# A softmax scale moved into the query norm, and a row maximum written out already negated

## The chip, the cores and the metric

The kernel runs on one core of one Trainium2 chip. The metric is the device time of one execution in microseconds (us). The profiled execution is one of its own, with its own time; the engines are named as in the profile: PE is TensorE (PEld its weight loads), DVE is VectorE, ACT is ScalarE, POOL is GpSimd, and SP issues most DMAs.

## The reference, cut to what matters

The model is two layers of a hybrid backbone on 256 latent and 256 context tokens of width 1024. Each layer has an input projection, four branches (Fourier, convolution, pooling, attention), a gated merge and an output projection, and then a feed-forward part (dense in layer 0, top 2 of 8 experts in layer 1). The change is in the attention branch alone:

```python
def rmsnorm(x, g):
    y = xf * lax.rsqrt(jnp.mean(xf * xf, axis=-1, keepdims=True) + EPS)
    return (y * g.astype(jnp.float32)).astype(x.dtype)
...
q = rmsnorm(proj[..., OFF_Q:OFF_K].reshape(b, l, N_HEADS, HEAD_DIM), q_norm_g)   # 8 heads of 64
...
def gqa_attend(qg, k, v):
    s = jnp.einsum('bqkgd,bskd->bkgqs', qg, k).astype(jnp.float32) * (HEAD_DIM ** -0.5)
    p = jax.nn.softmax(s, axis=-1).astype(v.dtype)
    return jnp.einsum('bkgqs,bskd->bqkgd', p, v)
```

Latent queries attend to 512 keys (256 latent, 256 context), context queries (layer 0 only) to the 256 context keys.

## The kernel before, in words

Every engine has one instruction stream, written out by hand in program order, and the streams meet through semaphores. Activations lie transposed (channels on partitions, tokens along the free dimension). The order of a layer's attention half is: norm1, the projections k, v, q0 to q3, F, ca, the head norms (`heads0` for k, `heads1` to `heads4` for q), more projections, rotary embedding, Fourier and pooling products, the duplication of the keys, then the attention units, then the four branches with their gates (`project("gate...")`, lines 556 to 558, and line 668), then the output projection. The eight PSUM banks are taken in a fixed rotation: `psum_order` writes down which result comes next, and a matmul that opens a bank waits until what lay in it eight places earlier has been read.

Head norm: PE sums the squares of a head (line 582), ACT takes the square root of mean plus eps (line 1012), DVE takes the reciprocal and multiplies q or k by it and by the gain (line 1355 and the two lines after it).

An attention unit is one head and one block of 128 query rows. There are 32 units in layer 0 (16 with 512 keys, then 16 with 256 keys) and 16 in layer 1 (all with 512 keys). For unit u:

- PE computes the scores S(u) into a bank (line 509). Units are issued in pairs. The two heads of a pair sit on different halves of the array's rows.
- DVE takes the row maximum (line 1410) into column 3 of a small tile `stat[:, u % 4]`, waits for its own result (`step`, a semaphore that DVE raises and waits for itself), multiplies it by -1/8 into column 0 (line 1411), and raises `negmax_ready`.
- ACT computes exp(S/8 + column 0) into `prob` or `root`, a ring of four buffers, with the row sum beside it (line 1040; the read of the accumulator is a second instruction).
- DVE takes the reciprocal of the row sum (line 1416), waits for itself, and scales the row (line 1417).
- PE transposes the row in blocks, T(u) (line 517). ACT copies the result to `pT` (line 1030, `keep_turned`).
- After four units PE multiplies by the values, V(v) (line 528), and DVE copies the result to `attnT` (line 1424, `keep_values`).

DVE's order is maximum(u), normalise(u - 1), and after every fourth unit keep_values. ACT's order is exp(u) and one keep_turned for each unit. PE's order is a pair of S, a V every second pair, a pair of T. The order of banks makes the second S of the pair that is issued after a V wait until DVE has copied that V out.

Constants lie in one tile `const`, whose columns are `ones`, `eps`, `ident`, `heads` and so on. It is loaded in two DMAs, the columns up to `eps` early and the rest later.

Of the kernel before, what the change touches and what calls it, by code (L numbers as in the profile page):

```python
# [16 lines left out]
ALU = mybir.AluOpType  # L17
ACT = mybir.ActivationFunctionType
AX = mybir.AxisListType.X
# [46 lines left out]

CONST = {}
_at = 0
for _name, _n in (("ones", P), ("eps", 1), ("ident", P), ("heads", P), ("rot", P), ("dup0", P), ("dup1", P), ("chan_cos", P),
                  ("chan_sin", P), ("pair", 2), ("below", P), ("iota", P), ("iota8", 8), ("seq", 2 * 512),  # L70
                  ("cos", LAT), ("sin", LAT)):
    CONST[_name] = (_at, _at + _n)
    _at += _n
# [50 lines left out]
def build(nc, xT_in, consts_in, pool_in, vec_in, cond_in, rows_in, router_in, first_in, mod_in, attn_in, ffn13_in, ffn2_in, moe_up_in, moe_down_in, out):  # L124
    with ExitStack() as ctx:
# [135 lines left out]
        def C(name):  # L261
            a, b = CONST[name]
            return const[:, a:b]
# [633 lines left out]
        def _(act):  # L897
# [96 lines left out]
            def attention_half(layer):  # L994
                N = T if layer == 0 else LAT
                if layer:
                    for n in range(2):
                        split(layer, n)
                norm(layer, "norm1", T)
                split(layer, 2)  # L1000
                for name in ("k", "v", "q0", "q1", "q2", "q3", "F0", "F1", "ca0", "ca1"):
                    if name in ("k", "q0", "q1", "q2", "q3"):
                        t = 0 if name == "k" else int(name[1]) + 1
                        n = T if t == 0 else N
                        b = filled(act, layer, name)
                        fn(hsq[:, t, 0:n], b[:, 0:n], ACT.Square).then_inc(S("head_square_ready"), 1)
                        fn(qk[:, t, 0:n], b[:, 0:n], ACT.Copy).then_inc(free(layer, name), 1)
                    split(layer, TILE_NO[name] + TILE_RING)
                for t in range(5):
                    n = T if t == 0 else N  # L1010
                    b = filled(act, layer, f"heads{t}")
                    fn(hsq[:, t, 0:n], b[:, 0:n], ACT.Sqrt, bias=C("eps"), scale=1.0 / HD) \
                        .then_inc(free(layer, f"heads{t}"), 1)
                for c in range(2):
                    b = filled(act, layer, f"cg{c}")
                    fn(sg[:, c, 0:N], b[:, 0:N], ACT.Sigmoid).then_inc(free(layer, f"cg{c}"), 1)
                    split(layer, TILE_NO[f"cg{c}"] + TILE_RING)
                for c in range(2):
                    split(layer, TILE_NO[f"P{c}"] + TILE_RING)

                units = attention_units(layer)

                def keep_turned(u):
                    s, g, qt, j = units[u]
                    n = 4 - 2 * s
                    v = u // 4
                    if j == 0 and v >= 2:
                        filled(act, layer, f"V{v - 2}")
                    b = filled(act, layer, f"T{u}")
                    fn(pT[:, v % 2, 0:n, j, :], b[:, 0:n * P].rearrange("p (c q) -> p c q", q=P), ACT.Copy) \  # L1030
                        .then_inc(free(layer, f"T{u}"), 1)

                for u in range(len(units) + 4):
                    if u % 2 and u >= 4:
                        keep_turned(u - 4)
                    if u < len(units):
                        n = T if units[u][0] == 0 else CTX
                        nxt("negmax_ready")
                        b = filled(act, layer, f"S{u}")
                        fn(probs[u % 4][:, 0:n], b[:, 0:n], ACT.Exp, bias=stat[:, u % 4, 0:1], scale=HD ** -0.5,  # L1040
                           accum_out=stat[:, u % 4, 1:2]).then_inc(free(layer, f"S{u}"), 1)
                    if u % 2 and 3 <= u < len(units) + 3:
                        keep_turned(u - 3)

                step = 0
                for i in BRANCH_ORDER:
                    if i == 1:
                        act.wait_ge(S("conv_summed"), layer + 1)
                        for c in range(2):
                            fn(csq[:, c, 0:N], conv[:, c, 0:N], ACT.Square).then_inc(S("conv_square_ready"), 1)  # L1050
                        b = filled(act, layer, "convnorm")
                        fn(root[:, 0:N], b[:, 0:N], ACT.Sqrt, bias=C("eps"), scale=1.0 / 256) \
                            .then_inc(free(layer, "convnorm"), 1)
                        for c in range(2):
                            nxt("conv_normed")
                            fn(conv[:, c, 0:N], conv[:, c, 0:N], ACT.Silu).then_inc(S("conv_ready"), 1)
                    for j in range(KD):
                        if step == 0:
                            act.wait_ge(S("conv_gated"), 2 * layer + 2)
                        if step >= 2:  # L1060

                            pi, pj = BRANCH_ORDER[(step - 2) // KD], (step - 2) % KD
                            read(act, layer, f"branch{pi}{pj}")
                        b = filled(act, layer, f"gate{i}{j}")
                        fn(sg[:, step % 2, 0:N], b[:, 0:N], ACT.Sigmoid).then_inc(free(layer, f"gate{i}{j}"), 1)  # L1065
                        split(layer, TILE_NO[f"gate{i}{j}"] + TILE_RING)
                        step += 1
                norm(layer, "norm2", N)
# [121 lines left out]
        def _(dve):  # L1190
# [137 lines left out]
            def attention_half(layer):  # L1328
# [78 lines left out]
                def maximum(u):  # L1407
                    n = T if units[u][0] == 0 else CTX
                    b = filled(dve, layer, f"S{u}")
                    step(dve.tensor_reduce(stat[:, u % 4, 3:4], b[:, 0:n], AX, ALU.max))  # L1410
                    ts(stat[:, u % 4, 0:1], stat[:, u % 4, 3:4], -HD ** -0.5, None, ALU.mult).then_inc(S("negmax_ready"), 1)

                def normalise(u):
                    n = T if units[u][0] == 0 else CTX
# [298 lines left out]
def constants():  # L1713

    c = np.zeros((P, CONST_LEN), np.float64)

    def put(name, a):
        c[:a.shape[0], CONST[name][0]:CONST[name][1]] = a

    i = np.arange(P)  # L1720
    put("ident", np.eye(P))
    put("ones", np.ones((P, P)))
    put("heads", (i[:, None] // HD == i[None, :] // HD).astype(float))

    rot = np.zeros((P, P))
    for out_c in range(P):
        rot[out_c + 16 if out_c % 32 < 16 else out_c - 16, out_c] = -1.0 if out_c % 32 < 16 else 1.0
    put("rot", rot)
    for g in range(NKV):
        d = np.zeros((P, P))  # L1730
        d[HD * g + i % HD, i] = 1.0
        put(f"dup{g}", d)
    ch = np.outer(np.arange(64), np.arange(64)) * (2 * np.pi / 64)
    eye2 = np.eye(2)
    norm = 1.0 / np.sqrt(64.0 * LAT)
    put("chan_cos", np.kron(eye2, np.cos(ch)) * norm)
    put("chan_sin", -np.kron(eye2, np.sin(ch)) * norm)
    put("pair", np.tile(np.eye(2), (2, 1)))
    put("below", (i[:, None] < i[None, :]).astype(float))
    put("iota", np.tile(i[None, :], (P, 1)))  # L1740
    put("iota8", np.tile(E - np.arange(E)[None, :], (P, 1)))
    put("eps", np.full((P, 1), EPS))
    t = np.outer(np.arange(LAT), np.arange(LAT)) % LAT * (2 * np.pi / LAT)
    s = np.concatenate([np.cos(t), np.sin(t)], axis=1).reshape(2, P, 512)
    put("seq", s.transpose(1, 0, 2).reshape(P, 1024))
    n_freq = HD // 4
    freqs = (10000.0 ** (-np.arange(n_freq) / n_freq)).astype(np.float32)
    tok = np.arange(LAT)
    where = np.where((i % HD < 32)[:, None], (tok // GRID_W)[None, :], (tok % GRID_W)[None, :])
    angle = where.astype(np.float32) * freqs[i % 16][:, None]  # L1750
    put("cos", np.cos(angle.astype(np.float64)))
    put("sin", np.sin(angle.astype(np.float64)))

    m = np.zeros((2, 2, P, 2, LAT))
    for g, w in enumerate(WINDOWS):
        full = np.zeros((LAT, LAT))
        for o in range(LAT):
            lo, hi = max(o - w // 2, 0), min(o + w // 2, LAT)
            full[lo:hi, o] = 1.0 / (hi - lo)
            full[o, o] -= 1.0  # L1760
        m[g // 2, :, :, g % 2, :] = full.reshape(2, P, LAT)
    pool = m.transpose(2, 0, 1, 3, 4).reshape(P, POOL_LEN)
    return c.astype(np.float32), pool.reshape(P, 2, 2, LAT * 2).astype(np.float32)
# [98 lines left out]
```

## Time and profile before

| | |
|---|---|
| median of 3 runs | 2235.92 us (2235.74 to 2236.14) |
| profiled execution: time | 2234.71 us |
| profiled execution: span, first to last instruction | 2232.9 us |
| mean granted TensorE clock over the span | 0.98 of full speed |
| instructions | 27842 |

The time of the profiled execution is its span and 1.8 us around it. A busy share is an average over stages. Which engine sets the pace of a stage is read from the chain of waits, which is followed back from the last instruction, and from the order of time on each engine. The granted clock is given as a share of 2.4 GHz, so 0.5 is 1.2 GHz.

### The profile page before, as it was taken

What the parts mean: (1) busy time and instruction counts of PE and PEld (TensorE: products, weight loads), DVE (VectorE), ACT (ScalarE), POOL (GpSimd) and SP (SyncE); (2) the same over time, 40 slices, a digit from 0 to 9 for tenths busy, and PEclk for the clock granted to TensorE, in tenths of its full rate; (3) what the DMA queues carried; (4) which work ended last, traced back from release to release, by engine and by line L of the source; (5) the groups of instructions that cost most, each with busy time, mean ns of one, the idle gap of its engine ahead of it and who ended that gap; (6) DMA issues with size and microseconds to landing.
All of it is one profiled execution on the core that took longest, in us unless ns stands there. A gap on an engine that the chain in (4) does not pass through costs nothing.

```text
span 2232.9 us, 27842 instructions
## 1 busy us (share of the span) xinstructions
PE 2135.7 (96%) x9866; PEld 1710.4 (77%) x9866; DVE 1713.1 (77%) x2158; ACT 1120.7 (50%) x1276; POOL 42.5 (2%) x84
## 2 busy tenths in 40 slices
PE   8989999998999999779997999999999999999997
PEld 6765776655788888667987888888888888888886
DVE  7777687646767766777745988988898988889895
ACT  3316221213333332434334777767777777767774
POOL 0000000000000000000000000000000000000000
PEclk9999999999999999899997999999999999999999
DMA  7500244343444443222444899989899999989993
GB/s 316 198 24 1 95 175 141 123 151 113 154 166 170 159 159 133 94 72 78 177 165 188 348 368 346 371 329 371 333 362 359 350 349 350 372 324 368 336 375 118
DMA packets 77284, 512.38 MB, mean 229 GB/s; under 512 B 8738, under 2 KB 9890, under 8 KB 22820
## 3 DMA queue, kind: packets, MB, share of 16 engines
q1 hardware_dynamic: 65700, 469.59, 55.9%
q0 software_dynamic: 11520, 41.95, 5.4%
q8 instruction: 38, 0.62, 0.1%
q14 instruction: 26, 0.21, 0.0%
HBM read 510.46 MB, written 1.05 MB: 229 GB/s over the span
## 4 chain that ended last, share of the span: by engine, by line
PE 88%; DVE 8%; ACT 2%; issue 2%; DMA 1%; SPq 0%; DVEq 0%; ACTq 0%
PE bank L807 9%; PE bank L805 9%; PE bank L806 9%; PE bank L556 5%; PE bank L558 5%; PE bank L557 5%; PE bank L668 5%; PE bank L826 5%; PE bank L828 5%; PE bank L827 5%; PE bank L678 4%; PE bank L724 2%; PE bank L725 2%; PE bank L726 2%; PE bank L700 2%; PE bank L710 2%
## 5 line engine op out<-in xcount | busy, mean ns | idle before, releaser
L934 ACT ACTIVATE down_high<-W 128x1024 fp32r<-128x1024 f32 x224 | 237.1, 1064 | 139.3 <-PE bank L828 139.2
L1275 DVE TENSOR_TENSOR up_b_low<-W,up_b_high 128x2048 fp32r<-128x2048 f32 x112 | 256.5, 2290 | 56.5 <-ACT up_b_high L927 56.5
L1282 DVE TENSOR_TENSOR down_low<-W,down_high 128x1024 fp32r<-128x1024 f32 x224 | 271.8, 1223 | 31.8 <-ACT down_high L934 22.5
L556 PE MATMUL bank<-h_high,tile_high 128*128 128x512 f32 (+1 forms) x704 | 259.7, 369 | 11.7 <-DVE tile_low L1326 11.7
L1269 DVE TENSOR_TENSOR up_a_low<-W,up_a_high 128x2048 fp32r<-128x2048 f32 x112 | 255.8, 2284 | 1.9 <-ACT up_a_high L921 1.9
L558 PE MATMUL bank<-h_high,tile_low 128*128 128x512 f32 (+1 forms) x704 | 239.3, 340 | 0.0
L557 PE MATMUL bank<-h_low,tile_high 128*128 128x512 f32 (+1 forms) x704 | 239.2, 340 | 0.0
L921 ACT ACTIVATE up_a_high<-W 128x2048 fp32r<-128x2048 f32 x112 | 212.9, 1901 | 2.1 <-PE bank L807 2.1
L927 ACT ACTIVATE up_b_high<-W 128x2048 fp32r<-128x2048 f32 x112 | 213.2, 1903 | 0.0
L826 PE MATMUL bank<-down_high,mact_high 128*128 128x512 f32 x448 | 186.4, 416 | 2.6 <-DVE down_low L1282 2.6
L828 PE MATMUL bank<-down_low,mact_high 128*128 128x512 f32 x448 | 176.3, 393 | 0.0
L805 PE MATMUL bank<-up_a_high,gathered_high 128*128 128x512 f32 x448 | 174.5, 390 | 1.4 <-DVE gathered_low L1603 1.4
L827 PE MATMUL bank<-down_high,mact_low 128*128 128x512 f32 x448 | 175.4, 392 | 0.0
L807 PE MATMUL bank<-up_b_low,gathered_high 128*128 128x512 f32 x448 | 175.0, 391 | 0.0
L805 PE MATMUL bank<-up_b_high,gathered_high 128*128 128x512 f32 x448 | 174.4, 389 | 0.3 <-DVE up_b_low L1275 0.3
L807 PE MATMUL bank<-up_a_low,gathered_high 128*128 128x512 f32 x448 | 174.3, 389 | 0.0
L806 PE MATMUL bank<-up_b_high,gathered_low 128*128 128x512 f32 x448 | 174.3, 389 | 0.0
L806 PE MATMUL bank<-up_a_high,gathered_low 128*128 128x512 f32 x448 | 174.3, 389 | 0.0
L556 PEld LDWEIGHTS bank<-h_high,tile_high 128*128 128x128 f32 x704 | 135.6, 193 | 35.2 <-DVE tile_low L1326 12.6
L1065 ACT ACTIVATE sg<-bank 128x512 f32<-128x512 f32 (+1 forms) x64 | 31.4, 490 | 261.2 <-PE bank L558 261.1
L557 PEld LDWEIGHTS bank<-h_low,tile_high 128*128 128x128 f32 x704 | 135.7, 193 | 21.9 <-issue 7.9
L558 PEld LDWEIGHTS bank<-h_high,tile_low 128*128 128x128 f32 x704 | 135.5, 192 | 14.7
(229 smaller groups left out, 4087.7 us busy)
## 6 DMA issues: line engine op xcount, KB each, us to landing
W<-in_moe_up SPq DMA_DIRECT2D x224, 1024.0 KB, 6.0
W<-in_moe_down SPq DMA_DIRECT2D x112, 1024.0 KB, 4.9
W<-in_w_mod_later POOLq DMA_DIRECT2D x80, 512.0 KB, 3.7
W<-in_ffn SPq DMA_DIRECT2D x33, 1024.0 KB, 4.8
W<-in_attn_blocks SPq DMA_DIRECT2D x24, 1280.0 KB, 5.9
W<-in_attn_blocks SPq DMA_DIRECT2D x22, 1024.0 KB, 5.2
W<-in_attn_blocks SPq DMA_DIRECT2D x8, 1536.0 KB, 7.1
shift_tiles<-in_w_mod_first SPq DMA_DIRECT2D x8, 512.0 KB, 13.9
```

The lines of the kernel that those rows point to most:

```text
L556: mm(b[:, 0:n], wh[:, r, k, :], hh[:, k, 0:n], start=k == 0, stop=False)
L557: mm(b[:, 0:n], wh[:, r, k, :], hl[:, k, 0:n], start=False, stop=False)
L558: last = mm(b[:, 0:n], wl[:, r, k, :], hh[:, k, 0:n], start=False, stop=k == KD - 1)
L805: mm(b[:, :], hgh[:, k, :], high[u][:, kk, :], start=k == 0, stop=False)
L806: mm(b[:, :], hgl[:, k, :], high[u][:, kk, :], start=False, stop=False)
L807: last = mm(b[:, :], hgh[:, k, :], low[u][:, kk, :], start=False, stop=k == KD - 1)
L826: mm(b[:, :], mah[:, u, a], ch[:, h, w], start=start and h == 0, stop=False, skip_group_check=True)
L827: mm(b[:, :], mal[:, u, a], ch[:, h, w], start=False, stop=False, skip_group_check=True)
L828: last = mm(b[:, :], mah[:, u, a], cl[:, h, w], start=False, stop=stop and h == 1, skip_group_check=True)
L1269: tt(al[u][:], raw_a[u].rearrange("p (k n) -> p k n", k=KD // 2), ah[u][:].bitcast(F32), ALU.subtract) \
L1275: tt(bl[u][:], raw_b[u].rearrange("p (k n) -> p k n", k=KD // 2), bh[u][:].bitcast(F32), ALU.subtract) \
L1282: tt(cl[:, h, :], raw_c[u][:, h * D:(h + 1) * D], ch[:, h, :].bitcast(F32), ALU.subtract) \
```

## The change

The factor 1/8 on the scores is taken into the queries. For the four q tiles the square root is taken of the sum of squares plus 64 eps, in place of the sum over 64 plus eps, which makes its reciprocal smaller by the factor 8. For this a constant column `eps_q` is added behind `eps`, so all constants behind it move by one column, and the second of the two DMAs of `const` is one column longer. The exponential has no scale any more. The row maximum is written negated by the reduction itself; the multiplication behind it and DVE's wait on its own semaphore between the two are gone. That is one instruction fewer for each of 48 units.

```diff
-for _name, _n in (("ones", P), ("eps", 1), ("ident", P), ...
+for _name, _n in (("ones", P), ("eps", 1), ("eps_q", 1), ("ident", P), ...
...
                 for t in range(5):
                     n = T if t == 0 else N
                     b = filled(act, layer, f"heads{t}")
-                    fn(hsq[:, t, 0:n], b[:, 0:n], ACT.Sqrt, bias=C("eps"), scale=1.0 / HD) \
+                    fn(hsq[:, t, 0:n], b[:, 0:n], ACT.Sqrt, bias=C("eps_q" if t else "eps"), scale=1.0 if t else 1.0 / HD) \
                         .then_inc(free(layer, f"heads{t}"), 1)
...
-                        fn(probs[u % 4][:, 0:n], b[:, 0:n], ACT.Exp, bias=stat[:, u % 4, 0:1], scale=HD ** -0.5,
+                        fn(probs[u % 4][:, 0:n], b[:, 0:n], ACT.Exp, bias=stat[:, u % 4, 0:1],
                            accum_out=stat[:, u % 4, 1:2]).then_inc(free(layer, f"S{u}"), 1)
...
-                    step(dve.tensor_reduce(stat[:, u % 4, 3:4], b[:, 0:n], AX, ALU.max))
-                    ts(stat[:, u % 4, 0:1], stat[:, u % 4, 3:4], -HD ** -0.5, None, ALU.mult).then_inc(S("negmax_ready"), 1)
+                    dve.tensor_reduce(stat[:, u % 4, 0:1], b[:, 0:n], AX, ALU.max, negate=True).then_inc(S("negmax_ready"), 1)
...
+    put("eps_q", np.full((P, 1), HD * EPS))
```

## Rows read from the trace of the kernel before

**Rows 1.** The page: busy time, share of the span, instructions of three engines.

```profile
PE 2135.7 (96%) x9866; PEld 1710.4 (77%) x9866; DVE 1713.1 (77%) x2158; ACT 1120.7 (50%) x1276; POOL 42.5 (2%) x84
```

**Rows 2.** The page: the chain that ended last, by engine.

```profile
PE 88%; DVE 8%; ACT 2%; issue 2%; DMA 1%; SPq 0%; DVEq 0%; ACTq 0%
```

**Rows 3.** Windows: start:end, length, busy us (count) by engine, PE clock, DMA share, GB/s.

```profile
163.00:212.00 49.00, 42.68 (x260) 23.56 (x257) 39.08 (x136) 34.97 (x97) 0.00 (x0) 1.00 0.01 1
997.00:1028.00 31.00, 26.15 (x159) 14.88 (x156) 22.58 (x67) 21.53 (x49) 0.00 (x0) 0.94 0.00 1
```

**Rows 4.** Timeline of DVE, layer 0, a unit of 512 keys: start, us, engine, line, operation.

```profile
166.50 0.68 DVE L1410 TENSOR_REDUCE stat<-bank 128x1 f32<-128x512 f32 x1
167.22 0.15 DVE L1411 TENSOR_SCALAR stat<-stat 128x1 f32<-128x1 f32 x1
167.29 0.15 DVE L1416 RECIPROCAL stat<-stat 128x1 f32<-128x1 f32 x1
167.48 0.49 DVE L1417 TENSOR_SCALAR prob<-prob,stat 128x512 f32<-128x512 f32 x1
167.88 0.68 DVE L1410 TENSOR_REDUCE stat<-bank 128x1 f32<-128x512 f32 x1
```

**Rows 5.** Chain of waits, layer 0, up to the first V: start, us, what.

```profile
166.59 0.61 DVE stat L1410
...
172.11 0.61 DVE stat L1410
...
173.71 0.50 ACT pT L1030
```

**Rows 6.** Chain of waits, layer 0, from the first V to the end.

```profile
179.50 1.99 PE bank L509 x4
...
206.17 0.16 DVE stat L1411
...
208.94 0.94 ACT pT L1030 x3
```

**Rows 7.** Timeline of DVE, layer 0: a copy of V, then a unit of 256 keys.

```profile
179.89 0.41 DVE L1424 COPY attnT<-bank 128x256 f32<-128x256 f32 x1
180.23 0.68 DVE L1410 TENSOR_REDUCE stat<-bank 128x1 f32<-128x512 f32 x1
...
191.59 0.42 DVE L1410 TENSOR_REDUCE stat<-bank 128x1 f32<-128x256 f32 x1 [0.84 <-PE bank L509]
...
192.12 0.15 DVE L1416 RECIPROCAL stat<-stat 128x1 f32<-128x1 f32 x1
```

**Rows 8.** Timeline of ACT, layer 0, three instructions in a row.

```profile
183.99 0.60 ACT L1030 ACTIVATE pT<-bank 128x512 f32<-128x512 f32 x1 [0.70 <-PE bank L517]
184.48 0.68 ACT L1040 ACTIVATE prob<-bank,stat 128x512 f32<-128x512 f32 x1
...
185.14 0.60 ACT L1030 ACTIVATE pT<-bank 128x512 f32<-128x512 f32 x1
```

**Rows 9.** Timeline of PE, layer 0 and then layer 1: eight blocks of T in each.

```profile
176.32 1.09 PE L517 MATMUL bank<-const,prob 128*128 128x128 f32 x8
...
1002.16 2.03 PE L517 MATMUL bank<-const,prob 128*128 128x128 f32 x8
1004.12 1.60 PE L509 MATMUL bank<-kdup,qk 64*128 64x512 f32 x4
```

**Rows 10.** Windows, layer 1, columns as in rows 3.

```profile
1002.00:1006.00 4.00, 4.00 (x17) 2.28 (x16) 3.79 (x13) 3.31 (x9) 0.00 (x0) 0.61 0.00 0
```

**Rows 11.** Timeline of DVE, then chain of waits, both of layer 1.

```profile
1005.76 0.69 DVE L1410 TENSOR_REDUCE stat<-bank 128x1 f32<-128x512 f32 x1
...
1019.96 0.16 DVE stat L1411
```

**Rows 12.** Instructions by line: duration ns min/median/max, first and last start, forms.

```profile
L647 PE MATMUL bank<-qk,const x8: 379/523/592, 397.7 to 1125.7; 128*128 128x512 f32 x4, 128*128 128x256 f32 x4
L582 PE MATMUL bank<-hsq,const x20: 379/592/592, 101.8 to 958.0; 128*128 128x512 f32 x12, 128*128 128x256 f32 x8
```

More of the change, by code:

```diff
@@ L68 @@
 _at = 0
-for _name, _n in (("ones", P), ("eps", 1), ("ident", P), ("heads", P), ("rot", P), ("dup0", P), ("dup1", P), ("chan_cos", P),
+for _name, _n in (("ones", P), ("eps", 1), ("eps_q", 1), ("ident", P), ("heads", P), ("rot", P), ("dup0", P), ("dup1", P), ("chan_cos", P),
                   ("chan_sin", P), ("pair", 2), ("below", P), ("iota", P), ("iota8", 8), ("seq", 2 * 512),
```

## The prediction

> **What bounds the kernel now.** I read the page first. PE is busy for 96% of the span and DVE for 77% [rows 1], and the chain that ended last runs over PE for 88% and over DVE for 8% [rows 2]. So a faster DVE is worth only what it saves in stretches where the chain runs over the changed instructions. These run in two stretches alone, layer 0 from 163 to 212 us and layer 1 from 997 to 1028 us, 80 us of 2232.9 [rows 3]. In neither is an engine full: PE is busy 42.68 of 49 us and DVE 39.08 [rows 3]. The question is therefore which engine is late at each joint, and for that I went to the timeline of each engine and to the chain of waits within the two stretches.
>
> **What one unit saves on DVE.** In steady state the reduction starts at 166.50, the multiplication at 167.22, the reciprocal at 167.29, the scaling of the row at 167.48 and the next reduction at 167.88, which makes a period of 1.38 us [rows 4]. The multiplication starts 0.04 after the reduction has ended (166.50 + 0.68 = 167.18), because DVE waits for its own result. An instruction that waits for nothing starts before the one ahead of it has ended: the reciprocal 0.08 early (167.22 + 0.15 = 167.37 against 167.29), the reduction 0.09 early [rows 4], and behind a copy out of PSUM 0.07 early (179.89 + 0.41 = 180.30 against 180.23) [rows 7]. After the change the reciprocal of unit u - 1 stands directly behind the reduction of unit u and does not depend on it. From start to start that is 0.79 now and will be 0.68 - 0.08 = 0.60: 0.19 us less. For 256 keys it is 192.12 - 191.59 = 0.53 now [rows 7] and 0.42 - 0.08 = 0.34 after, again 0.19. No row shows a reduction with a waitless successor, so I bound this from both sides. At the least the slot of the multiplication goes, 167.29 - 167.22 = 0.07. At the most 0.79 - 0.60 and a little more, 0.23, if the successor could start 0.12 early. I take 0.19, by the nearest row, the copy out of PSUM. The path to ACT gains about as much: from the start of the reduction to the end of the multiplication it is 0.87 now and will be 0.68, and the wait behind it stays, which I count as 0.18.
>
> The Trainium skill has a rule that speaks against this size. VectorE: DVE Perf Modes, section The DRAIN you can't avoid, says that an instruction costs its pipeline flush with or without a semaphore, and that the semaphore itself costs nothing extra. By that rule the removed wait is worth nothing, and the sum would be the 1.1 us of the first rival below. The rows here differ: 0.04 late with the wait, 0.07 to 0.09 early without [rows 4, 7]. The same page says elsewhere that an instruction which isn't held starts earlier.
>
> **Where the segment is on the path, layer 0.** From the end of the ACT table load the chain is DVE's own loop. Five reductions stand on it before the first V, the first at 166.59 and the last at 172.11 [rows 5]. The last hands over to ACT, whose copy at 173.71 releases V [rows 5]. Savings: 4 x 0.19 + 0.18 = 0.94. DVE's period becomes 1.38 - 0.19 = 1.19. ACT must keep up: copy to exp takes 184.48 - 183.99 = 0.49 and exp to copy 185.14 - 184.48 = 0.66, together 1.15 [rows 8]. That is just under 1.19, so ACT is next in line but not yet the bound. PE needs for two units, without a V, some 1.06 for a pair of S and 1.09 for eight blocks of T [rows 9], 2.15 against DVE's 2.38, and is hidden too.
>
> From the first V on PE is the bound for most of each group of four units, and DVE sits idle for 0.84 us in each [rows 7]. But the chain crosses DVE once in every group. The pair of S that comes after V takes 1.99 at 179.50 where a pair takes 1.06 [rows 6], because its second half waits for the bank that DVE empties with the copy at 179.89 [rows 7]. That copy stands behind the reduction, the multiplication, the reciprocal and the scaling of the row. Each such crossing gives 0.19. There are five (V1 to V5): 0.95. V6 is released over DVE's line 1411 (206.17 [rows 6]) and ACT: 0.17. V7 is released by three ACT copies at 208.94 [rows 6] and gives nothing. Layer 0: 0.94 + 0.95 + 0.17 = 2.06.
>
> **Layer 1.** The loop before the first V looks the same but is not. PE's clock is at half there: 0.61 between 1002 and 1006 [rows 10], a stretch at 1.2 GHz that follows PE's long wait for the first row. Eight blocks of T take 2.03 us in place of 1.09, and the next pair of S 1.60, without a gap between them [rows 9], and the reduction at 1005.76 has just waited for that pair [rows 11]. What DVE gains earlier is lost in waiting for PE. Only the last segment, from that reduction over ACT to V0, keeps its 0.18. V1 has the crossing of layer 0 (0.19), V2 is released over line 1411 (1019.96 [rows 11]) and ACT (0.18), V3 by ACT alone. Layer 1: 0.55.
>
> **The other edits.** The square root and the exponential keep their instruction, shape and count, with other constants: 0. I see no row with such a constant changed; a table with another cost would be the only way, and both take their scale as an immediate before and after. The constants move from odd to even columns. `heads` (now odd, column 257) is multiplied in at most 592 ns and `ones` (even, column 0), in the same shape, in at most 592 ns [rows 12], so I take 0 between ends of -0.1 and +0.1 us. The DMA of the constants grows by one column in 2698, 0.04% of it, and all DMAs together are 1% of the chain, 22 us [rows 2]: under 0.01 us. No wait is added, no transfer is moved. After attention the chain is PE's own gate projections, so what is saved moves everything behind it forward by as much.
>
> **Sum.** 2.06 + 0.55 = 2.61 us, 14 segments of 48. The profiled execution took 2234.71, so 2232.1 by its own measure. It lies 1.21 under the median of the runs, 2235.92, so the forecast is **2233.3 us**.
>
> **Rivals.**
> - *Only the slot is won.* If a successor of the reduction starts no earlier than the multiplication does now, each segment gives 0.07 to 0.08: 14 x 0.075 = 1.05, so 2234.9. For it: a reduction may keep its pipe longer than a copy. Against it: three different pairs of rows all start early [rows 4, 7].
> - *The clock falls elsewhere.* PE waits as long for the first row in layer 0, with the clock at 1.00 throughout [rows 3]. If the stretch at half clock comes in both layers, layer 0 loses four of its five first steps, 0.76: 2234.1. If it comes in neither, layer 1 gains them: 2232.5. Everything behind layer 0 also runs 2 us earlier, and the other half-clock stretches may come out a little longer or shorter, about a microsecond either way.
> - *DVE was the pace all along.* 48 x 0.19 = 9.1, so 2226.8. Against it: DVE's idle 0.84 [rows 7] and the copies of ACT on the chain [rows 6].
> - *The reduction gets slower by the negation.* This is the one way to the other side. Place: line 1410. Price, if a second pass is made: (0.68 - 0.42) / 256 [rows 4, 7] is 1.0 ns an element, 0.52 us for 512 keys and 0.26 for 256. Net of the 0.19 it is +0.33 and +0.07. Layer 0: 5 x 0.33 before the first V, 2 x 0.33 and 4 x 0.07 after; layer 1: 5 x 0.33, as DVE then is slower than PE even at half clock, and 2 x 0.33. That is 2.6 + 2.3 = 4.9, so 2240.8. It decides from a reduction of 0.68 + 0.19 = 0.87 us on. Nothing in the trace shows a negated reduction.
>
> **Chances.** The forecast 0.60, only the slot 0.12, the clock 0.12, DVE all along 0.04, slower 0.04, nothing 0.08. The range of 8 in 10 goes from 2230.9 (0.23 a segment is 3.2, no half clock in layer 1 another 0.8, one later half-clock stretch shorter by 1.0) to 2236.0 (only the slot and one such stretch longer, or nothing arrives). This kernel's runs can tell a change of about 0.2%, that is 4.5 us: faster means under 2231.4, slower over 2240.4. Faster: 0.04 from DVE all along and 0.04 from the low ends of the forecast and the clock, 0.08. Slower: 0.04. Within: 0.88.
>
> **What would show it.** Right: no row on line 1411's place, the reduction still at 0.68 and 0.42, a period of 1.19 before the first V of layer 0, the reciprocal 0.60 behind the start of the reduction, V0 of layer 0 about 0.94 earlier against the first exp, V to V shorter by 0.19, ACT nearly without gaps in the first loop, and layer 1 shorter by 0.5. Wrong: a reduction over 0.7 us, a first loop with a period of 1.3 or more, a stretch at 0.5 of the clock within 163 to 212 us, or a difference behind the attention that isn't the shift alone.

## The result, and the profile after

The changed kernel takes 2229.98 us (median of 9 runs, 2228.42 to 2230.91), the kernel before 2235.74 us on the same chip (9 runs, 2233.26 to 2237.15). The ratio is 0.9976, with a 95% interval of 0.9967 to 0.9985: 5.8 us less, where 2.6 were forecast. The time lies under the range. The profiled execution took 2230.79 us, with a span of 2229.0, against 2234.71 and 2232.9 before.

On VectorE the change does to the rows what the working said. The page of the kernel after, busy time and the chain by engine, against rows 1 and 2:

```profile
PE 2137.6 (96%) x9866; PEld 1714.5 (77%) x9866; DVE 1706.0 (77%) x2110; ACT 1119.7 (50%) x1276; POOL 42.6 (2%) x84
...
PE 89%; DVE 7%; ACT 2%; issue 1%; DMA 1%; SPq 0%; DVEq 0%; ACTq 0%
```

DVE has 48 instructions fewer and 7.1 us less to do. The timeline of DVE in layer 0, the same unit as in rows 4 (line 1415 is now the reciprocal, 1416 the scaling of the row):

```profile
165.95 0.68 DVE L1410 TENSOR_REDUCE stat<-bank 128x1 f32<-128x512 f32 x1
166.55 0.15 DVE L1415 RECIPROCAL stat<-stat 128x1 f32<-128x1 f32 x1
166.74 0.49 DVE L1416 TENSOR_SCALAR prob<-prob,stat 128x512 f32<-128x512 f32 x1
167.14 0.69 DVE L1410 TENSOR_REDUCE stat<-bank 128x1 f32<-128x512 f32 x1
```

The negated reduction still takes 0.68 us, the reciprocal starts 0.60 behind it, and the period is 1.19 against 1.38 [rows 4]. So the size of one segment, 0.19 us, was right. The difference lies elsewhere: in where the clock fell and in the loop over the experts. The chain of waits of the kernel before (start, us, what) is shown at its first S and last V of each layer and its first V of layer 0, at the gathers (the products that collect an expert's tokens, line 760) for the second and the third expert, and at the last one:

```profile
162.62 1.11 PE bank L509 x3
...
174.44 1.95 PE bank L528 x16
...
210.12 1.08 PE bank L528 x8
...
996.30 1.11 PE bank L509 x3
...
1026.07 1.95 PE bank L528 x16
...
1329.56 3.57 PE bank L760 x32
...
1454.61 3.57 PE bank L760 x32
...
2204.93 3.57 PE bank L760 x32
```

The same of the kernel after:

```profile
162.07 1.11 PE bank L509 x3
...
173.74 1.95 PE bank L528 x16
...
208.30 1.08 PE bank L528 x8
...
994.43 1.11 PE bank L509 x3
...
1023.60 1.95 PE bank L528 x16
...
1327.32 3.57 PE bank L760 x32
...
1452.12 3.57 PE bank L760 x32
...
2200.96 3.57 PE bank L760 x32
```

From the first S to the last V, layer 0 takes 46.23 us in place of 47.50 (1.27 less, 2.06 expected) and layer 1 29.17 in place of 29.77 (0.60 less, 0.55 expected). Then comes what the prediction does not have. One turn of the loop over the experts takes 1452.12 - 1327.32 = 124.80 us and took 125.05 before. The change touches none of its instructions. Over the seven turns that can be read, from the second gather to the last, that is 1.73 us. If the first expert gains as much, it is 2.0 over eight; its own stretch can't show it, as a half-clock stretch of the router reaches into it (before, a granted clock of 0.61 from 1211 to 1214 us, with the first gather at 1209.60).

The 3.92 us between the two profiled executions are these: 0.55 ahead of the first S, where the change has nothing that it should shorten, 1.27 in layer 0's attention, 0.60 in layer 1's, 1.73 in the seven turns, and -0.23 in all the rest.

Layer 0 lost its first steps to the clock. A window of the kernel after, columns as in rows 3, just as T and S of the first units run:

```profile
166.00:170.00 4.00, 3.91 (x16) 2.29 (x16) 3.82 (x11) 2.83 (x8) 0.00 (x0) 0.63 0.00 0
```

The granted clock is 0.63 there, so part of these 4 us ran at 1.2 GHz; in the first profile of the kernel before it was 1.00 throughout layer 0's attention [rows 3]. PE had waited for the first row just before, 2.03 us against 2.04 there. The prediction named such a stretch as a sign of being wrong; it belongs to its rival on the clock.

### The profile page after: what moved, and what is told of

Same layout as the page of the kernel before. It is cut to its first block, busy times and chain, and to the rows that moved or that the text cites. A ratio compares the mean times of both kernels' runs of the same rounds, so it can differ in the third digit from the quotient of the medians.

```text
span 2229.0 us, 27794 instructions
## 1 busy us (share of the span) xinstructions
PE 2137.6 (96%) x9866; PEld 1714.5 (77%) x9866; DVE 1706.0 (77%) x2110; ACT 1119.7 (50%) x1276; POOL 42.6 (2%) x84
## 4 chain that ended last, share of the span: by engine, by line
PE 89%; DVE 7%; ACT 2%; issue 1%; DMA 1%; SPq 0%; DVEq 0%; ACTq 0%
PE bank L805 9%; PE bank L807 9%; PE bank L806 9%; PE bank L556 5%; PE bank L557 5%; PE bank L558 5%; PE bank L668 5%; PE bank L826 5%; PE bank L828 5%; PE bank L827 5%; PE bank L678 4%; PE bank L724 2%; PE bank L725 2%; PE bank L726 2%; PE bank L709 2%; PE bank L699 2%
```

## The experiments

Below, "one expert" is the time between two gathers in a chain of waits. Theory A: the gain beyond the attention comes from the constants, which moved from odd to even columns. Theory B, the rival: the place of the constants does nothing, and the rest is the phase of the loop (how its waits fall against each other), or chance. The first four kernels tell these apart.

**e1, only the columns moved.** The kernel before with an unused `eps_q` behind `eps`.

```diff
-("ones", P), ("eps", 1), ("ident", P), ("heads", P), ...
+("ones", P), ("eps", 1), ("eps_q", 1), ("ident", P), ("heads", P), ...
```

> The kernel before with the column eps_q added behind eps and not used: every constant behind it moves from an odd to an even column, nothing else changes. Measured is 5.8 us less for the whole change, while the attention stretches account for 1.9 us in the trace and the loop over the experts for 1.8 us (125.05 us for one expert before, 124.80 after). Theory A (the constants' columns make PE's transposes in the expert loop a little faster): 125.05 becomes about 124.80, the run 1.5 to 3 us shorter than before. Theory B (the place of the constants does nothing; the rest is phase and scatter): within 0.7 us of before, one expert still takes 125.05.

2233.49 us against 2235.82, ratio 0.9988 (0.9979 to 0.9997). Its chain of waits, the same two gathers:

```profile
1330.29 3.57 PE bank L760 x32
...
1455.09 3.57 PE bank L760 x32
```

124.80 us for one expert, with all of VectorE's work unchanged. Theory A holds and B falls for this part: by the runs the columns alone are worth 2.3 us (0.7 to 4.7), by the seven turns in the trace 1.73.

**e2, the change without the move.** `eps_q` as the last constant.

```diff
-("eps", 1), ("eps_q", 1), ("ident", P), ...
+("eps", 1), ("ident", P), ...
...
-("cos", LAT), ("sin", LAT)):
+("cos", LAT), ("sin", LAT), ("eps_q", 1)):
```

> The whole change, but with eps_q as the last constant, so that all others keep their odd columns. Theory A: only the attention's part is left, 2 to 3 us less than before (2233), and one expert takes 125.05 us. Theory B: like the change itself, 5 to 6 us less (2230), and 124.80 us for one expert, if that comes from the removed instructions by way of the phase in which the loop runs.

2231.81 us, ratio 0.9983 (0.9974 to 0.9992): 4.0 us less, more than theory A's 2 to 3, with a wide interval. One expert takes 125.05 us again (1326.60 and 1451.65 in its chain). So the columns decide the loop and not the removed instructions.

**e12, the same kernel once more**, because of that interval.

> The change with eps_q as the last constant, once more, as the first time gave a wide interval (2231.8, 4.0 us less than before). By the terms read from the traces it should give 1.9 to 3.3 us in the attention stretches and up to 0.7 in the router's stage, 2.0 us less than the change itself with its moved constants: 2231.5 to 2233.

2231.78 us against 2235.24, ratio 0.9987 (0.9978 to 0.9996). In both sets of runs the negated reduction by itself is worth 3.5 to 4 us, with intervals that reach from 0.9 to 5.8. The chain of waits of e12, layer 1's first S and last V, then the output projection and the first gather:

```profile
995.22 1.11 PE bank L509 x3
...
1023.60 1.95 PE bank L528 x16
...
1156.01 27.91 PE bank L678 x128
...
1206.34 5.85 PE bank L760 x32
```

Layer 1's attention takes 28.38 us here, 1.39 less than before, as the half clock does not fall within it. The stage of the router, from the output projection to the first gather, takes 50.33 where the kernel before needs 51.11 (1158.49 to 1209.60). No instruction in it has changed. Both chains are alike up to the router's first products, 33.18 us into the stage. The first of these, and the window of 2 us around it, in the kernel before and then in e12:

```profile
1191.67 0.99 PE bank L737 x4
```

```profile
1191.60:1193.60 2.00, 1.93 (x10) 1.96 (x11) 2.00 (x6) 2.00 (x6) 0.00 (x0) 0.50 1.00 418
```

```profile
1189.19 0.58 PE bank L737 x4
```

```profile
1189.10:1191.10 2.00, 1.91 (x14) 1.94 (x14) 2.00 (x6) 2.00 (x6) 0.00 (x0) 0.74 1.01 426
```

Before, these products run at half clock from the first on. In e12 the clock is still at 1.00 for the first of them (1189 to 1190 us) and falls behind it. PE has waited for ScalarE just ahead in both, 3.56 and 3.57 us. After 1.4 us of such products e12 is 0.79 ahead, and 0.78 at the end of the stage. But what layer 0 saves (46.30 in place of 47.50) is not in this profile's total, as a table further down shows.

**e3 and e4, the change and the kernel before once more.**

> The change once more, unaltered, as the yardstick for the other runs on this chip: theory B's scatter would let its expert period and its half-clock stretch in layer 0's attention come out otherwise than in the first profile; if both are fixed by the kernel, the profile shows 124.80 us again. Time 2230 +- 1.

> The kernel before, unaltered, timed against itself: within 0.7 us of before by every theory. It shows in a second profile whether 125.05 us for one expert and the clock at full speed throughout layer 0's attention belong to the kernel or to one execution.

e3: 2230.08 us, ratio 0.9975 (0.9966 to 0.9984). e4: 2235.10 us, ratio 0.9998 (0.9989 to 1.0007). One expert takes 124.80 and 125.05 us again: both belong to the kernels. The half clock in layer 0's attention does not. In e4 the window from 166 to 170 us shows 0.58 in a kernel that had 1.00 in its first profile. V0 stands 11.92 us behind the first S in place of 11.82, so the half clock costs the kernel before next to nothing there, where DVE sets the pace.

These two and the kernels of the other experiments show what the stretches outside the attention do. Microseconds between marks of the chains of waits (start of the first S, start of the last V, second gather, last gather):

| | before | e4 | after | e3 | e12 | e10 | e7 |
|---|---|---|---|---|---|---|---|
| up to the first S | 162.62 | 162.04 | 162.07 | 161.47 | 161.35 | 161.64 | 163.55 |
| attention, layer 0 | 47.50 | 47.61 | 46.23 | 46.29 | 46.30 | 46.32 | 45.45 |
| up to layer 1's first S | 786.18 | 786.22 | 786.13 | 787.49 | 787.57 | 787.53 | 786.29 |
| attention, layer 1 | 29.77 | 29.68 | 29.17 | 28.53 | 28.38 | 29.69 | 28.53 |
| up to the second gather | 303.49 | 304.27 | 303.72 | 302.81 | 302.88 | 304.30 | 302.70 |
| seven experts | 875.37 | 875.37 | 873.64 | 873.65 | 875.38 | 875.37 | 873.93 |

In e3, e12 and e10 the stretch between the two attentions is 1.3 us longer than in the kernel before, and what layer 0's attention had saved is gone when layer 1's begins. In these three the granted clock is 0.57 or 0.58 both from 404 to 412 and from 985 to 989 us; the kernel before has 0.74 and 1.00 there, e4 0.81 and 0.61. No instruction in that stretch has changed. That the clock makes the difference is read from its place and not tested. The time up to the first S differs by up to 2.2 us as well.

**e5 and e6, which constant.** One unused column on both sides of `ident` (e5), or behind it (e6), in the kernel before.

```diff
-("eps", 1), ("ident", P), ("heads", P), ...
+("eps", 1), ("pad0", 1), ("ident", P), ("pad1", 1), ("heads", P), ...     # e5
+("eps", 1), ("ident", P), ("pad0", 1), ("heads", P), ...                  # e6
```

> The kernel before, with one unused column ahead of ident and one behind it: ident moves to an even column (130), all other constants stay at odd ones. Theory A1 (PE's transposes in the expert loop read ident, and its column decides): one expert takes 124.80 us as in the two kernels with all constants moved, the time is about 2 us less than before. Theory A2 (another constant decides): 125.05 us, no difference.

> The kernel before, with one unused column behind ident: ident stays at column 129, all constants behind it move to even columns. Theory A1 (ident decides): 125.05 us for one expert and no difference in time (within 0.8 us). Theory A2: 124.80 us and about 2 us less.

e5: 2233.62 us against 2235.00, ratio 0.9991 (0.9982 to 1.0001). e6: 2234.95 us, ratio 0.9997 (0.9988 to 1.0007). The two times are near the limit of what can be told. The traces are not. The two gathers in the chains of e5, then of e6:

```profile
1330.25 3.57 PE bank L760 x32
...
1455.05 3.57 PE bank L760 x32
```

```profile
1329.85 3.57 PE bank L760 x32
...
1454.90 3.57 PE bank L760 x32
```

124.80 with `ident` alone moved, 125.05 with all the others moved. The constants' tile is as long in e6 as in e1 (124.80), so it isn't its length either. It is the column of `ident` that counts, and the only reader of `ident` in the seven turns is line 814, PE's transposes. The other profiles agree: the ten kernels and repeats with `ident` at column 129 take 875.4 us each for seven experts, the five with it at column 130 873.6. In the runs the same step is 1.7 us between e2 and e3, taken together, and 1.6 between e14 and e13 below.

**e7, the change with `ident` on a multiple of 64 bytes** (14 more unused columns).

> The change, with 14 unused columns behind eps_q, so that ident starts at column 144, a multiple of 64 bytes, instead of 130. If only odd or even counts: 124.80 us for one expert and the time of the change (2230.0 +- 0.7). If coarser alignment counts too, less than 124.80 us for one expert, and each 0.1 us there makes 0.8 us in all.

2229.50 us, ratio 0.9971 (0.9959 to 0.9983), 124.85 us for one expert: nothing more from the coarser alignment, and no faster than the change within the intervals. But this profile has the clock at 1.00 from 166 to 170 us. Its chain, first S, first V and last V of layer 0:

```profile
163.55 1.11 PE bank L509 x3
...
174.44 1.95 PE bank L528 x16
...
209.00 1.08 PE bank L528 x8
```

V0 stands 10.89 us behind the first S, 0.93 less than before (0.94 expected), and the whole takes 45.45 in place of 47.50: 2.05 less, where the prediction has 2.06. From the third unit on the chain before V0 runs over ACT, with a copy every 1.19 us (170.12, 171.32, 172.51), so ACT is level with DVE here, and a still faster DVE would win nothing in this loop.

**e15, a second identity for the expert loop alone**, at an even column at the end of the constants, in the kernel before.

```diff
-mprod[:, u, h * P:(h + 1) * P], C("ident"))
+mprod[:, u, h * P:(h + 1) * P], C("ident2"))
```

> The kernel before with a second identity at an even column (2828) at the end of the constants, read only by the transposes in the expert loop (line 814); all others read the old one at column 129. Theory A1 in its narrow form (the transposes of the expert loop alone pay for the odd column): one expert 124.80 us and the run about 2 us less than before. If another reader of ident pays: 125.05 us.

2234.36 us against 2234.99, ratio 1.0000 (0.9990 to 1.0009), and 124.95 us for one expert (1328.07 and 1453.02 in its chain). That is between the two values, so neither form of the theory is met. Line 814 alone, in a window of 245 us of the loop (PE busy, then its weight loads, clock, DMA share, GB/s), in the kernel before, e5 and e15:

```profile
1460.00:1705.00 245.00, 10.30 (x54) 7.54 (x54) 1.00 0.93 352
```

```profile
1460.00:1705.00 245.00, 10.24 (x54) 7.46 (x54) 1.00 0.92 352
```

```profile
1460.00:1705.00 245.00, 10.26 (x54) 7.46 (x54) 1.00 0.92 353
```

The weight loads of the transposes are as short in e15 as in e5. So the transposes do pay for the odd column, but they are the smaller part. An expert is 14 turns of an inner loop, and a turn is 18 ns shorter in e5 than before. By the starts of PE's products between 1460 and 2200 us some 6 of these lie at the two transposes of a turn (108.3 ns from one to the next in place of 110.5), in e15 too (108.4). The other 12 or so lie between the products of the down projection behind them (lines 826 to 828), which don't read `ident`; in e15 they gain only 1. The second identity also moves everything behind the constants by 129 columns, rounded. Why those products follow the column of `ident`, and why not in e15, stays open.

**e8, the scale alone.** The maximum taken plainly, then multiplied by -1.

```diff
-dve.tensor_reduce(stat[:, u % 4, 0:1], b[:, 0:n], AX, ALU.max, negate=True).then_inc(S("negmax_ready"), 1)
+step(dve.tensor_reduce(stat[:, u % 4, 3:4], b[:, 0:n], AX, ALU.max))
+ts(stat[:, u % 4, 0:1], stat[:, u % 4, 3:4], -1.0, None, ALU.mult).then_inc(S("negmax_ready"), 1)
```

> Half of the change: the scale goes into the query norm (square root with eps_q, exponential without a scale), but the maximum is taken plainly and multiplied by -1 on VectorE in a second instruction, as before. eps_q is the last constant, so no constant moves. All theories: the norm and the exponential cost what they cost, so DVE's period before the first V is 1.38 us, the steps from V to V are those of before (6.97, 6.55, 5.72, 5.28, 4.42, 4.06 us in layer 0), the time is within 0.8 us of before. If it is shorter by over 1 us, the scale itself pays in a way that I missed.

2235.22 us, ratio 1.0002 (0.9992 to 1.0011), DVE's period 1.38 us. Square root and exponential with other constants cost nothing that shows, as predicted.

**e9, the wait kept, the multiplication gone.**

```diff
 dve.tensor_reduce(stat[:, u % 4, 0:1], b[:, 0:n], AX, ALU.max, negate=True).then_inc(S("negmax_ready"), 1)
+done_max[0] += 1
+dve.wait_ge(S("negmax_ready"), done_max[0])
```

> The change without the multiplication but with VectorE's wait kept: behind the negated reduction VectorE waits for that reduction's own semaphore before it goes on. eps_q is the last constant, so the constants stay at odd columns. Theory W (the wait costs most of the 0.19 us): only the slot of the multiplication is saved, the reciprocal starts 0.72 us behind the start of the reduction, DVE's period before the first V is 1.31 us, each step from V to V is 0.07 us shorter than before and not 0.19, the attention gives 1.0 us in all. Theory N (a wait on one's own semaphore costs nothing, as the Trainium skill's page VectorE: DVE Perf Modes, section The DRAIN you can't avoid, has it): 1.19 us and 0.19 as in the change.

The timeline of DVE in layer 0 (lines shifted by up to 3):

```profile
165.76 0.68 DVE L1411 TENSOR_REDUCE stat<-bank 128x1 f32<-128x512 f32 x1
166.48 0.16 DVE L1418 RECIPROCAL stat<-stat 128x1 f32<-128x1 f32 x1
166.68 0.49 DVE L1419 TENSOR_SCALAR prob<-prob,stat 128x512 f32<-128x512 f32 x1
167.08 0.69 DVE L1411 TENSOR_REDUCE stat<-bank 128x1 f32<-128x512 f32 x1
```

The reciprocal starts 0.72 behind the reduction, the period is 1.32. So of 0.19 us the multiplication's slot makes 0.06 and the wait on its own semaphore 0.13. The Trainium skill's VectorE: DVE Perf Modes, section The DRAIN you can't avoid, has it, measured on a chain of copies, that such a semaphore costs nothing extra; by the rows here it cost 0.13 us each. The attention stretches are 0.83 and 0.40 us shorter than before (161.81 to 208.48, 991.63 to 1021.00), 1.2 together, about the 1.0 expected.

The time, though, is 2229.73 us, ratio 0.9976 (0.9966 to 0.9986): 5.5 us less, with the constants at odd columns and 125.05 us for one expert. Neither theory had that.

**e14 and e13, the same once more, and with `eps_q` behind `eps`.**

> The negated reduction with VectorE's own wait kept and the constants at odd columns, a second time. If the placement of the half-clock stretches belongs to the kernel: 2229.7 +- 0.7 again, and the stretch near 560 us is 3.4 us long and not 6.8, and two of 6.8 stand between 900 and 920 where other kernels have 3.4, 3.4 and 6.8. If it was luck: 2234 to 2234.6, 1.0 us less than before.

> The negated reduction with VectorE's own wait kept, now with eps_q behind eps as in the change, so that ident is at its even column. By sums: the kernel with the wait and odd columns took 5.4 us less than before, though its attention stretches are only 1.2 us shorter; its trace lays the rest on half-clock stretches that fall elsewhere. If that placement belongs to the kernel and survives a start that is a little different, 2.0 us come on top for the expert loop (124.80 us each): 2227.7, faster than the change. If it was the luck of one set of executions, about 2232.5 (2235.4 - 1.0 - 2.0).

e14: 2230.53 us against 2234.99, ratio 0.9984 (0.9975 to 0.9993). The gain, 4.5 us, is less than the first time but more than the attention's 0.9 (0.50 and 0.37 in this profile). The placement is as the first theory had it: the granted clock is 0.50 from 559.1 to 562.3 and back at 1.00 from 562.6 on, and 0.50 throughout 900.6 to 907.1 and 910.8 to 917.3. e13: 2228.91 us, ratio 0.9975 (0.9965 to 0.9985), between what its two theories expected. The gain is not the luck of one set. From the last V of layer 0 to the first S of layer 1, where no instruction differs, e9 takes 783.15 us, e14 and e13 781.69 each, the kernel before 786.18 and 786.22. The chain of waits of the kernel before, from the last product of the third branch over the wait for the norm of the convolution to the output projection; then of e14:

```profile
394.40 3.45 PE bank L668 x8
...
408.65 3.78 PE bank L668 x4
...
465.54 55.22 PE bank L678 x128
```

```profile
392.89 3.45 PE bank L668 x8
...
407.14 1.98 PE bank L668 x4
...
461.11 55.22 PE bank L678 x128
```

And two windows of each, the kernel before first:

```profile
408.00:411.00 3.00, 2.35 (x3) 1.18 (x4) 0.00 (x0) 2.97 (x4) 0.00 (x0) 0.50 0.02 5
411.00:416.00 5.00, 5.00 (x14) 3.39 (x13) 3.43 (x4) 0.45 (x1) 0.00 (x0) 0.64 0.00 0
```

```profile
408.00:411.00 3.00, 3.00 (x12) 2.07 (x11) 1.74 (x3) 1.93 (x3) 0.00 (x0) 1.00 0.02 5
411.00:416.00 5.00, 5.00 (x21) 3.57 (x19) 3.19 (x5) 1.33 (x2) 0.53 (x1) 1.00 0.07 16
```

The stage takes 68.22 us in e14 and 71.14 before, 2.92 less. In both PE waits for VectorE and ScalarE; before it comes back to a clock of 0.50, in e14 to 1.00, and four products take 1.98 in place of 3.78. The work is the same. What differs is when the wait comes, by 1.5 us, and the clock behind it; that the one decides the other is argued. The kernel before doesn't always take 71.14 us for it either: in e4 it is 69.88.

**e10 and e11, the negated reduction in one layer alone.**

```diff
+if layer == 0:      # e11: layer == 1
     dve.tensor_reduce(..., ALU.max, negate=True).then_inc(S("negmax_ready"), 1)
+else:
+    step(dve.tensor_reduce(...)); ts(..., -1.0, None, ALU.mult).then_inc(S("negmax_ready"), 1)
```

> The negated reduction in layer 0's 32 units alone; layer 1 takes the maximum plainly and multiplies it by -1. The constants stay at odd columns. If the gain is that of the stretch itself: from the first S to the last V of layer 0 47.0 us in place of 48.2 to 48.3 where PE's clock is at half in it, 46.2 where it is not; the run 1.3 to 2.1 us less than before. If the earlier arrival also changes where the half-clock stretches fall behind it, the stage from layer 1's output projection to the first gather is 50.4 us in place of 51.1, and the run is 2 to 3 us less.

> The negated reduction in layer 1's 16 units alone, constants at odd columns. From the first S to the last V of layer 1 30.0 us in place of 31.3, or 30.7 where the half clock falls within it; layer 0 keeps 48.2 to 48.3; the run 0.6 to 1.3 us less than before, and up to 0.7 more if the router's stage shortens to 50.4 too.

e10: 2233.83 us against 2235.24, ratio 0.9991 (0.9982 to 1.0001). Layer 0 takes 46.32 us from first S to last V, with the half clock in it, and the router's stage stays at 51.12. e11: 2233.65 us, ratio 0.9992 (0.9983 to 1.0001). Layer 1 takes 28.38 us, and the router's stage 50.37. The expectations count the stretches from other marks (48.2 for what is 47.5 here); as differences, 1.2 to 1.3 us were expected of each. The runs, 1.4 and 1.6 us less, can't be told from nothing: both intervals include 1. In e10's profile the 1.2 us of layer 0 are lost before layer 1 begins (table above), and from the first S to the second gather it takes 1167.84 us against 1167.78 in e4. e11 takes 1165.28 there.

## Why the prediction was wrong

**The step that failed** is the one on the other edits: that the constants move from odd to even columns was costed at 0, between -0.1 and +0.1 us. It is worth -2.0 us: 0.25 us for each expert, read in seven of the eight (e1, e5 against e6). The prediction tested it against two rows of other readers, the products with `heads` and `ones` [rows 12], and these do not show it; the rows that matter were 112 turns of a loop that it took to be untouched, each with two transposes that read `ident`. With a term of 2.0 the sum is 4.6 and the forecast 2231.3. That is still 1.3 over the measured 2229.98.

**Right: the size of a segment.** 0.68 for the reduction, 0.60 to the reciprocal, a period of 1.19, 0.19 a segment. The rival of a slower reduction is refuted by the 0.68. The prediction read "no second pass" out of the Trainium skill, Vector Engine (DVE) Microarchitecture Reference, section 2.3, which states only that the sign is a constant set by the handler; the row bears the reading out. The rival of the slot alone is refuted by the period: with the wait kept (e9) it is 1.32, without it 1.19.

**Right: where it stands in layer 0.** Steps from V to V (174.44 to 181.49 before, 173.74 to 180.60 after) shrink by 0.18 to 0.20, V5 to V6 by 0.17, and V6 to V7 by 0.01. The sum, 2.06, is met to 0.01 where the clock stays at full speed (e7). In the five other profiles without the own wait (after, e2, e3, e10, e12) the half clock falls in the first loop, PE becomes the bound, and 1.2 to 1.3 are left. That was the rival on the clock, with -0.76.

**Failed as well: what is saved moves everything behind it forward.** In e3, e10 and e12 the 1.2 to 1.3 us of layer 0 are gone at the first S of layer 1, and e2 (787.49 between the attentions) is like them. In the first profile of the changed kernel and in e7 they are kept.

**Mis-sized: layer 1.** 0.55 holds, V by V (0.21, 0.20, 0.19 and nothing), for the one profile with the half clock within the stretch. In e2, e3, e7, e11 and e12 it is not, and the gain is 1.24 to 1.39. The rows of before showed one execution of two kinds, and I took it for the kernel.

**Mis-sized: the other half-clock stretches.** "About a microsecond either way" is too little. One of them goes with 2.9 us in the stage behind the convolution's norm (e14), another with 0.8 in the router's (e12).

The account: the measured 5.8 are 2.0 for `ident` and, by e2 and e12, 3.5 to 4.0 for the negated reduction, where 2.6 were forecast. In e12's profile the latter are not the terms of the prediction. Against e4 it is 3.4 us shorter: 0.7 ahead of the first S, nothing between the first S of layer 0 and that of layer 1 (1.3 saved, 1.3 lost), 1.3 in layer 1's attention and 1.4 from there to the second gather. So that the runs' 3.5 to 4.0 has the size of the forecast 2.6 is in part luck. No profile shows the whole 5.8: the first of the changed kernel lies 3.9 under that of the kernel before, e3 5.0 under e4. The rest lies in executions that were not profiled. That it too comes from the clock is argued from e9 and e14 and not shown. Why `ident` costs in the expert loop and shows nothing from V to V in the attention is open as well.

## What to carry to other kernels

When a constant is inserted, every address behind it in its tile moves: cost that for each reader in the longest loop, and put new constants at the end if only the edit is to be timed. When an engine's wait on its own result goes, count the wait (0.13 us here) and not only the instruction (0.06). Where PE has waits of some microseconds between full stretches, a small saving ahead of them may come out smaller (e10) or larger (e14) behind them, so check the granted clock of each stage in more than one profile before you call a stretch the kernel's.

## What the runs showed of the hardware

- The column of a 128x128 fp32 identity read by PE's transposes changes an expert's time from 125.05 (column 129) to 124.80 us (column 130) and 124.85 (column 144); the first two hold for ten and five profiles. That it is odd against even, and not these columns alone, isn't shown. A third of the difference lies at the transposes, the rest between the products behind them.
- A reduction that writes its maximum negated takes 0.68 us for 512 elements, as the plain one does (kernels after and before).
- A VectorE instruction behind a reduction out of PSUM that it doesn't wait for starts 0.08 us before the reduction's end; behind a wait for it, 0.04 after (kernel after and e9).
- A kernel with 0.9 to 1.2 us less in its attention ran 5.5 and 4.5 us faster in two sets of runs (e9, e14). In e14 the clock is 1.00 from 408 to 416 us, where the kernel before has 0.50 and 0.64.
